# Two heads of a recurrent scan normed and gated at a time inside the scan's rounds, with half of a projection moved into its first rounds

## The reference, cut to what matters

```python
y_c, states_c = rwkv_scans(r_c, v_c, dirs_c, (zero, zero))   # both directions, 8 heads of 64
y_l, _ = rwkv_scans(r_l, v_l, dirs_l, states_c)
def rwkv_out(y, r, v, dirs, g, prm):
    mean = jnp.mean(y, axis=-1, keepdims=True)               # over the 64 of a head
    var = jnp.mean(jnp.square(y - mean), axis=-1, keepdims=True)
    yn = ((y - mean) * lax.rsqrt(var + LN_X_EPS)).reshape(B, L, RW_DIM) * prm['ln_w'] + prm['ln_b']
    bonus = jnp.sum(r * k_sum * prm['r_k'], axis=-1, keepdims=True) * v
    return ((yn + bonus.reshape(B, L, RW_DIM)) * g).astype(g.dtype)
out_l = jnp.concatenate([rwkv_out(...), o_l], axis=-1) @ prm['w_out']   # the same for the context
```

## Time and profile before

| | us |
|---|---|
| median of 3 runs (lowest, highest) | 2639.47 (2636.53, 2642.45) |
| the profiled execution, its own time | 2644.11 |
| its span in the profile | 2642.2 |
| PE, VectorE, ScalarE (ACT), GpSimd (POOL) busy, share of the span | 91%, 66%, 40%, 13% |
| granted TensorE clock, mean | 0.951 |

### The profile page before, as it was taken

The page is one execution under the profiler, slowest core; times in us unless marked ns, Lnnn a source line. Parts: engine busy times, 40 slices in busy tenths (PEclk is TensorE's granted clock), DMA queues, the critical chain, the costliest instruction groups (busy, mean ns, idle before and its releaser), DMA issues.

```text
span 2642.2 us, 38711 instructions
## 1 busy us (share of the span) xinstructions
PE 2392.0 (91%) x15040; PEld 1770.8 (67%) x15040; DVE 1755.9 (66%) x3346; ACT 1047.5 (40%) x2030; POOL 354.1 (13%) x541
## 2 busy tenths in 40 slices
PE   7899999799989799899998799987899998998996
PEld 3788888554878799633454577774477775767775
DVE  4775786576746788722757566665568884647886
ACT  4222222233331444411134243432357873346884
POOL 1111100110000211000200233331012210001220
PEclk9899999899999799999998799998989999998998
DMA  7555654241326478311010000000269993215995
GB/s 284 183 203 196 215 199 144 93 143 64 123 85 207 158 274 289 132 56 56 32 40 32 25 3 3 2 3 1 96 212 347 334 314 131 72 53 190 337 330 198
DMA packets 115062, 386.97 MB, mean 146 GB/s; under 512 B 20160, under 2 KB 22336, under 8 KB 114624
## 3 DMA queue, kind: packets, MB, share of 16 engines
q1 hardware_dynamic: 76640, 276.33, 29.8%
q0 software_dynamic: 34848, 95.47, 10.7%
q10 hardware_dynamic: 3392, 12.70, 1.2%
HBM read 389.66 MB, written 26.21 MB: 157 GB/s over the span
## 4 chain that ended last, share of the span: by engine, by line
PE 35%; DVE 14%; DMA 8%; ACT 6%; issue 3%; POOL 0%; DVEq 0%; ACTq 0%; SPq 0%; POOLq 0%
PE ps L143 34%; DMA RG<-in_w 6%; DVE moe1wl L152 2%; DVE moe0wl L152 2%; DMA AR<-in_a 2%; PE ps L146 1%; DVE f2wl L152 1%; ACT moe1wh L149 1%; ACT moe0wh L149 1%; DVE rwXX L152 1%; DVE rwMM L172 1%; DVE H L160 1%; DVE acc L160 1%; ACT rwa L149 1%; ACT f2wh L149 1%
## 5 line engine op out<-in xcount | busy, mean ns | idle before, releaser
L143 PE MATMUL ps<-H,RG 128*128 128x256 f32 (+2 forms) x1088 | 364.1, 491 | 14.0 <-ACT H L149 14.0
L160 DVE SCALAR_TENSOR_TENSOR acc<-AR,cs,acc 128x512 f32<-128x512 f32 x420 | 295.4, 746 | 48.8 <-DMA AR<-in_a 46.0
L143 PEld LDWEIGHTS ps<-H,RG 128*128 128x128 f32 (+1 forms) x1088 | 206.4, 193 | 156.2 <-issue 140.1
L152 DVE TENSOR_TENSOR moe0wl<-RG,moe0wh 128x1024 fp32r<-128x1024 f32 x144 | 173.2, 1219 | 44.1 <-ACT moe0wh L149 33.8
L149 ACT ACTIVATE moe0wh<-RG 128x1024 fp32r<-128x1024 f32 x144 | 150.9, 1061 | 75.4 <-DMA RG<-in_w 42.8
L199 POOL DMA_DIRECT2D AR<-in_a x152 | 82.1, 541 | 658.0 <-DVE acc L160 503.1
L152 DVE TENSOR_TENSOR moe1wl<-RG,moe1wh 128x1024 fp32r<-128x1024 f32 x120 | 144.4, 1219 | 26.9 <-ACT moe1wh L149 22.2
L149 ACT ACTIVATE f1wh<-RG 128x1024 fp32r<-128x1024 f32 x66 | 69.7, 1061 | 230.7 <-PE ps L143 230.6
L143 PE MATMUL ps<-f1hh,f1wh 128*128 128x512 f32 x352 | 142.9, 406 | 8.0 <-DVE f1hl L152 8.0
L149 ACT ACTIVATE moe1wh<-RG 128x1024 fp32r<-128x1024 f32 x120 | 126.1, 1060 | 49.7 <-DMA RG<-in_w 30.2
L143 PE MATMUL ps<-f1hl,f1wh 128*128 128x512 f32 x352 | 141.5, 402 | 0.0
(11 more groups left out here) (643 smaller groups left out, 5834.0 us busy)
## 6 DMA issues: line engine op xcount, KB each, us to landing
RG<-in_w SPq DMA_DIRECT2D x525, 512.0 KB
AR<-in_a POOLq DMA_DIRECT2D x152, 512.0 KB, 3.9
moe0back<-moe_outs ACTq DMA_DIRECT2D x4, 1024.0 KB, 8.0
CT<-in_consts ACTq DMA_DIRECT2D x1, 2546.0 KB, 12.6
X<-in_x ACTq DMA_DIRECT2D x1, 2048.0 KB, 11.7
moe_rows<-moe0ht POOLq DMA_DIRECT2D x4, 512.0 KB, 5.0
moe1back<-moe_outs ACTq DMA_DIRECT2D x2, 1024.0 KB, 5.9
X<-in_ctx ACTq DMA_DIRECT2D x1, 1024.0 KB, 5.7
```

Of the source, the lines that this page charges most:

```text
L143: return Silent() if self.e is None else self.e.matmul(out, lhs, rhs, start=start, stop=stop, skip_group_check=True)
L152: return Silent() if self.e is None else self.e.tensor_tensor(out, a, b, op)
L160: return Silent() if self.e is None else self.e.scalar_tensor_tensor(out=out, in0=a, scalar=s, in1=b, op0=op0, op1=op1)
```

## The change

- **Start.** `out1` is split: columns 0 to 3 stay ahead of the scan, columns 4 to 7 are multiplied by PE in rounds 0, 1, 2 and 4 and added by VectorE in rounds 1, 2, 3 and 5. The terms of the bonus are made by VectorE in round 0, its products in round 8, its multiplications in round 9. POOL no longer waits for `out1`.
- **Storage.** `ST` and the `MM` of set 1 get space of their own. In each set `EI` shares its space with `T1` and `KB` with `XX`; the masks and one `T1` go to the end of `rwa` and to `nv`. VectorE's first write into `XX` waits for ACT's copy of `kbt`.
- **Closing.** Each pair of heads is normed and gated in the rounds after its last unit, from rounds 146, 159, 165 and 175 on, one operation a round (`close_pe`, `close_act`, `close_dve`); for the last pair VectorE's operations follow each other in round 177. All squares are ACT's; the root table is loaded in round 157. The rounds end at 179 instead of 175.
- **Second outputs.** The router's part moves to rounds 149 and 150. In rounds 175 to 177 the first four columns of `out2` get their products of the first three pairs of heads (`late_pe`); the fourth follows after the scan (`led_pe`), then columns 4 to 7.

```diff
     NS, APART = 4, 5
+    CLOSE = [146, 159, 165, 175]
...
-        self.ST = self.OM[:, 0:2, :].rearrange("p d (j n) -> p d j n", j=4)
-        size = dict(EB=[P, 129], EI=[P, P], RA=[P, 256], KB=[P, 2, P], KBt=[P, 2, P], MM=[P, 2, 512], WU=[P, 2, P],
-                    XF=[P, 2, P], XX=[P, 2, 2, 64], T1=[P, 2, 64], sm=[P, 2])
+        self.ST = g.sb(st, "rwst", [P, 2, 4, P])
+        size = dict(EB=[P, 129], RA=[P, 256], KBt=[P, 2, P], MM=[P, 2, 512], WU=[P, 2, P], XF=[P, 2, P], XX=[P, 2, 2, 64],
+                    T1=[P, 2, 64], sm=[P, 2])
...
-            self.sets.append({k: g.sb(st, f"rw{k}{i}", s) for k, s in size.items() if i > 1 or k != "MM"})
-        self.sets[1]["MM"] = self.OM[:, 2:4, :]
+            self.sets.append({k: g.sb(st, f"rw{k}{i}", s) for k, s in size.items() if i < 3 or k != "T1"})
+        self.sets[3]["T1"] = g.NV[:, 384:512].rearrange("p (a n) -> p a n", a=2)
         for B in self.sets:
             B["MC"], B["ML"] = (B["WU"][:, q, :].rearrange("p (h n) -> p h n", h=2) for q in range(2))
-        self.LC = [g.sb(st, f"rwlc{d}", [P, len(LEVELS) - 1, 64]) for d in range(2)]
-        self.IC = g.sb(st, "rwic", [P, 64])
+            B["EI"] = B["T1"].rearrange("p a n -> p (a n)")
+            B["KB"] = B["XX"].rearrange("p q h n -> p q (h n)")
+        self.LC = [x.rearrange("p (l n) -> p l n", n=64) for x in (self.A[:, at:at + 384], g.NV[:, 0:384])]
+        self.IC = self.A[:, at + 384:at + 448]
...
-        self.run(e, self.unit_pe)
-        for f in range(4):
-            ps = g.banks.take(("rw mean", f))
-            for tok in g.banks.free(("rw mean", f)):
-                e.wait_ge(*tok)
-            e.wait_ge(*S.dve.at("scanned"))
-            e.matmul(ps[:, :], g.C("avg64"), self.YB[:, f, :], True, True).then_inc(*p.up(("mean", f)))
-        self.nyb.pe(e)
-        g2, tok_g = g.ws.tile(("rw_g2_2", ix, (0, P), (0, T)), P, T)
-        e.wait_ge(*tok_g)
-        for f in range(4):
-            ps = g.banks.take(("rw g2", f))
-            for tok in g.banks.free(("rw g2", f)):
-                e.wait_ge(*tok)
-            e.matmul(ps[:, :], g2[0][:, f * P:(f + 1) * P], self.SG[:, :], True, True).then_inc(*p.up(("g2", f)))
-        g.ws.settle("rw g2", p.now())
+        self.run(e, self.unit_pe, self.close_pe, amid)
...
-        self.nyb.act(e, [S.dve.at(("centred", 3))])
+        self.run(e, self.unit_act, self.close_act)
...
+    def bonus_terms_dve(self, e):
+        g, v, K = self.g, self.S.dve, self.K
+        e.wait_ge(*v.now())
+        e.tensor_tensor(K[:, :, :], self.KD[0][:, :, :], self.KD[1][:, :, :], ADD).then_inc(*v.up())
+        e.wait_ge(*v.now())
+        e.tensor_tensor(K[:, :, :], K[:, :, :], self.R[:, :, :], MUL).then_inc(*v.up())
+        e.wait_ge(*v.now())
+        e.tensor_tensor(K[:, :, :], K[:, :, :], bc(g.V("r_k", 0, 4), [P, 4, T]), MUL).then_inc(*v.up("bonus"))
...
     def pool(self, e):
-        for tok in needs:
-            e.wait_ge(*tok)
...
-        self.nyb.pool(e, [S.dve.at(("centred", 3))])
...
-    def run(self, e, unit):
-
-        running = []
-        for r in range(self.APART * (len(self.todo) - 1 + self.NS)):
+    def run(self, e, unit, close=None, beside=None):
+
+
+        running, closing = [], []
+        for r in range(self.CLOSE[-1] + 4):
...
+            if close is not None and r in self.CLOSE:
+                closing.append(close(e, self.CLOSE.index(r)))
+            for u in list(closing):
+                if next(u, "over") == "over":
+                    closing.remove(u)
+            if beside is not None:
+                beside(e, r)
+
+    def last(self, j):
+
+        return self.todo.index((3, 1, j))
+
+    def close_pe(self, e, j):
+
+        g, p, S, y = self.g, self.S.pe, self.S, self.YB[:, j, :]
+        ps = g.banks.take(("rw mean", j))
+        for tok in g.banks.free(("rw mean", j)):
+            e.wait_ge(*tok)
+        e.wait_ge(*S.dve.at(("out", self.last(j))))
+        e.matmul(ps[:, :], g.C("avg64"), y, True, True).then_inc(*p.up(("mean", j)))
+        yield from (None for _ in range((10, 3, 3, 1)[j]))
+        ps = g.banks.take(("rw squares", j))
+        for tok in g.banks.free(("rw squares", j)):
+            e.wait_ge(*tok)
+        e.wait_ge(*S.act.at(("square", j)))
+        e.matmul(ps[:, :], g.C("avg64"), self.squares[:, j, :], True, True).then_inc(*p.up(("squares", j)))
+        yield from (None for _ in range((5, 5, 5, 1)[j]))
+        if j == 0:
+            self.g2 = g.ws.tile(("rw_g2_2", (0,), (0, P), (0, T)), P, T)
+        w, tok_g = self.g2
+        e.wait_ge(*tok_g)
+        ps = g.banks.take(("rw g2", j))
+        for tok in g.banks.free(("rw g2", j)):
+            e.wait_ge(*tok)
+        e.matmul(ps[:, :], w[0][:, j * P:(j + 1) * P], self.SG[:, :], True, True).then_inc(*p.up(("g2", j)))
+        if j == 3:
+            g.ws.settle("rw g2", p.now())
+        yield
+
+    def close_act(self, e, j):
+        g, a, S = self.g, self.S.act, self.S
+        yield from (None for _ in range((2, 2, 2, 1)[j]))
+        e.wait_ge(*S.dve.at(("centred", j)))
+        e.activation(self.squares[:, j, :], self.YB[:, j, :], ACT.Square).then_inc(*a.up(("square", j)))
+        yield from (None for _ in range((9, 2, 2, 1)[j]))
+        if j == 0:
+            g.root_table(e)
+        e.wait_ge(*S.pe.at(("squares", j)))
+        e.activation(self.roots[:, j, :], g.banks.of(("rw squares", j))[:, :], ACT.Abs_reciprocal_sqrt,
+                     bias=g.C("eps64")).then_inc(*a.up(("root", j)))
+        yield
+
+    def close_dve(self, e, j):
+        g, v, S = self.g, self.S.dve, self.S
+        y, m, inv = self.YB[:, j, :], self.squares[:, j, :], self.roots[:, j, :]
+        apart = int(j < 3)
+        yield from (None for _ in range(apart))
+        e.wait_ge(*S.pe.at(("mean", j)))
+        e.wait_ge(*v.at(("out", self.last(j))))
+        e.tensor_tensor(y, y, g.banks.of(("rw mean", j))[:, :], SUB).then_inc(*v.up(("centred", j)))
+        g.banks.done(("rw mean", j), v.now())
+        yield from (None for _ in range((10, 3, 3, 2)[j]))
+        e.wait_ge(*S.act.at(("root", j)))
+        e.scalar_tensor_tensor(m, g.banks.of(("rw squares", j))[:, :], 64e-5, inv, ADD, MUL).then_inc(*v.up())
+        g.banks.done(("rw squares", j), v.now())
+        yield from (None for _ in range(apart))
+        e.wait_ge(*v.now())
+        e.scalar_tensor_tensor(m, m, -0.5, inv, MUL, MUL).then_inc(*v.up())
+        yield from (None for _ in range(apart))
+        e.wait_ge(*v.now())
+        e.scalar_tensor_tensor(inv, m, 1.5, inv, ADD, MUL).then_inc(*v.up())
+        yield from (None for _ in range(apart))
+        e.wait_ge(*v.now())
+        e.scalar_tensor_tensor(y, y, g.V("ln_w", j), inv, MUL, MUL).then_inc(*v.up())
+        yield from (None for _ in range(apart))
+        e.wait_ge(*v.now())
+        e.scalar_tensor_tensor(y, y, g.V("ln_b", j), self.V[:, j, :], ADD, ADD).then_inc(*v.up())
+        yield from (None for _ in range(apart))
+        e.wait_ge(*v.now())
+        e.wait_ge(*S.pe.at(("g2", j)))
+        e.tensor_tensor(self.R[:, j, :], y, g.banks.of(("rw g2", j))[:, :], MUL).then_inc(*v.up(("r", j)))
+        g.banks.done(("rw g2", j), v.now())
+        yield
 
...
+                e.wait_ge(*S.act.at(("kbt", n)))
...
+        self.amid = [0, 1, 2, 4]
...
-        for f in range(KT):
-            if f == KT - 2:
-                self.rwkv.bonus_pe(e)
+        for f in range(4):
             self.out1.one_pe(e, f)
+
+    def amid_pe(self, e, r):
+
+        if r in self.amid:
+            self.out1.one_pe(e, self.amid.index(r) + 4)
+        if r == 8:
+            self.rwkv.bonus_pe(e)
+        self.late_pe(e, r)
+
+    def late_pe(self, e, r):
+
+        if r == 149:
+            self.router.pe(e, 0)
+        if r == self.rwkv.CLOSE[3]:
+            self.lead = {}
+        if r >= self.rwkv.CLOSE[3]:
+            for f in {0: [0], 1: [1, 2], 2: [3], 3: []}[r - self.rwkv.CLOSE[3]]:
+                self.lead[f] = self.out2.bank(e, f)
+                for k in range(3):
+                    self.lead_one_pe(e, f, k)
+
+    def lead_one_pe(self, e, f, k):
+        s = self.out2.specs(f)[k]
+        w, tok = self.g.ws.tile(s[:4], s[4], s[5])
+        e.wait_ge(*tok)
+        e.wait_ge(*self.rwkv.S.dve.at(("r", k)))
+        return e.matmul(self.lead[f], w[0], self.rwkv.R[:, k, :], k == 0, k == 3)
+
+    def led_pe(self, e):
+        p = self.S.pe
+        for f in range(4):
+            self.lead_one_pe(e, f, 3).then_inc(*p.up(("out", f)))
+        self.g.ws.settle((self.S.name, "out", 3), p.now())
+
+    def late_dve(self, e, r):
+        if r == 150:
+            self.router.dve(e, 0)
+            self.out2.gate_dve(e)
 
     def attended_dve(self, e):
         self.out1.gate_dve(e)
         e.wait_ge(*self.SO.dve.now())
-        for f in range(KT):
-            if f == KT - 2:
-                self.rwkv.bonus_dve(e)
+        for f in range(4):
             self.out1.one_dve(e, f)
+
+    def amid_dve(self, e, r):
```

(73 more changed lines are left out.)

## The result

The changed kernel takes 2613.34 us (median of four runs, 2609.39 to 2615.44), the kernel before in the same comparison 2638.01 (four runs, 2636.53 to 2642.45): ratio 0.9898, 95% interval 0.9879 to 0.9916, so about 1% faster. The profiled execution of after took 2615.44 us, span 2613.6.

A forecast was written before the change was run, and what follows sets the result against it. PE was taken to bound the kernel. Start 9.4 gained, closing in the rounds 8.5 lost and behind the scan 25.3 gained make 26.2 us, so 2613.3 us beside 2639.5; range 2603 to 2627 (8 in 10).

The forecast's parts named there:

- Start: Ahead of the scan and in its first rounds: splitting out1 fills PE's hole; 9.4 us gained, bounds 5 and 15.
- POOL hidden: Ahead of the scan: POOL's masks and clearings, 5.9 us, are covered by other engines' work.
- the bonus: In round 8: four bonus products on PE, taken in full at 3.6 us lost.
- the clock's return: Units 1 to 5: PE is throttled less after a shorter idle stretch; 2.0 us gained.
- Closing in the rounds: Norm and gate of the first three pairs inside the scan's rounds: 8.5 us lost, bounds 4 and 17.
- the allotment: Closing inside the rounds: loss summed from separate engine terms, PE 3.2 and 2.2, router 0.6, DVE 1.3, ACT 1.2 us.
- Behind the scan: From last mean to the end of out2: PE stays the bound without stalls; 25.3 us gained, bounds 23 and 27.
- Squares between exponentials: ACT's squares from round 148: no table load of their own, 0 taken, 2.6 us kept for the range.
- the slower rival: In each of 32 units DVE's first write into XX waits for ACT's kbt copy: 2645 us, chance 0.03.
- Rival 1: In the scan's rounds: the closing is fully seen, 18 us lost instead of 8.5; 2623 us, chance 0.17.
- Rival 3: First units: the clock does not fall, 4.8 more; scan's end hides closing products, 3; 2606 us, chance 0.15.
- rival 2: First rounds: the early start brings nothing, bonus products double if the clock stays at half; 2623 us, chance 0.10.

The follow-up runs named there:

- no_bonus: Changed kernel with the four bonus products and their multiplications left out (bonus missing from the output): 2606.31 us, ratio 0.9862 to the kernel before.
- thin_all: Changed kernel with the first three pairs' closing products and DVE and ACT operations on 64 columns in place of 512: 2609.49 us, ratio 0.9894 to before.
- Experiment 2: Four variants of the changed kernel, the first three pairs' closing partly left out or thinned on PE, on DVE and ACT, or on all: ratios 0.9886 to 0.9904 to before.
- start_only: Kernel before with only the change's first rounds and storage; norm, gate and second outputs stay behind the scan: 2633.65 us, ratio 0.995 to before.

## Why the prediction was right, and where it was not

The total (2613.3 against 2613.34) is closer than its terms deserve, and that is luck. The gain was put at 26.2 us and measured at 24.7; the other 1.5 us are the median of before, 2639.5 in the prediction and 2638.0 beside the result. Of the three terms the two gains were put 1.1 us too small each and the loss 3.5 too small.

- **Start, 9.4 predicted, 10.5 measured.** The first level product 11.0 us early: 11.3. POOL hidden: yes. But the bonus was counted at 3.6 and costs 6.9, and the clock's return at 2.0 where 6.1 came (17.4 at unit 28 in no_bonus less 11.3). I had bounded the bonus by hiding (0) and by doubling at half clock (7.2) and taken the middle. The size came near the upper bound, but not by that road: the block itself ran at 1.00 in 3.60 us, and the price lies in what it holds up and in the clock behind it. Two terms missed by 3 and 4 us with opposite signs, so the 9.4 is near by luck; other traces of the same rounds have unit 28 up to 4.2 us earlier still. Units 1 to 5 took 46.6 us, just outside the 41 to 46 I gave.
- **Closing in the rounds, 8.5 predicted, 12.0 measured** (10.5 ahead at unit 28, 1.5 behind at the last mean). This is the mis-sized term. 8.5 of it are lost at full clock up to "last full"; that this equals the 8.5 predicted for the whole closing is chance. The other 3.5 lie behind, where the clock is at half for 6.8 us and the third pair's three Newton operations, its last two and its gate product (2.02 us, at 1827.68) stand among the last unit's. PE waits there behind the Newton operations:

```profile
1823.55 0.69 PE L143 MATMUL ps<-rwXX,rwMM 64*64 64x64 f32 x4 [1.33 <-DVE rwXF L152]
```

With all of that thinned (thin_all) 3.3 of the 3.5 come back. The step that failed is the allotment: PE's products 5.4, DVE 1.3, ACT 1.2, router 0.6 as separate terms. Experiment 2 shows that they can't be summed: PE's alone give back 2.5, DVE's and ACT's alone 2.3, both 5.9 of 8.5. DVE with ACT was put too low; of ACT's 1.2 for load and root the load makes 0.2, and of the router's 0.6 there is 0.2.
- **Behind the scan, 25.3 predicted, 26.4 measured.** PE full, no stall, the led fourths 13.0 us behind the mean (three led products stand ahead of them in the group at 1841.58) where I had 13.4. What I had a little high is the product: 39 of them took 33.6 us, 0.86 each, at full clock; my 0.89 held a slow head.
- **The side notes.** The Trainium skill's price for a switch of table, 2.66 us with a drain of 1.38 in it (ScalarE: Activation LUTs, What ACT_TABLE_LOAD costs), was set against the trace: the load took 1.28 us at 1794.66, right behind the activation ahead of it (1794.37, 0.28 us), the idle activation began at 1795.96, and no drain of 1.38 shows on either side. Squares between exponentials need no load: none stands in rounds 148 to 156. `XX` never waits for the `kbt` copy, so the slower rival had nothing to act on.
- **Rivals.** Rival 1 was half right: more of the closing was seen. Rival 3 had the size of the clock's return (6.1 instead of 2.0, with no bonus in the rounds), but its condition did not hold in after, where the clock was at 0.50 for 13.7 us, and a bonus as dear as in rival 2 took the gain back. Rival 2's outcome did not come: the start brought 10.5 us.

## What to carry to other kernels

Where rounds tie PE, DVE and ACT together, don't price added work as a share per engine: measure with all of it thinned, then one engine at a time. Here the single numbers summed to 4.8 us where both together gave 5.9. Try work moved out of a hole spread over the thin rounds one instruction at a time, not set down as a block: here that made four products free that cost 4.3 to 6.9 us as a block. And count marks from the last operation that both kernels share, for executions drift by more than the terms in question.

## What the runs showed of the hardware

TensorE's clock fell with PE never idle for long: in after it went from 1.00 to 0.50 at about 1495.7, and in the 6 us ahead of it PE was busy 3.28 us with 1.84 us as the longest wait. With the four products spread, PE was busy 4.99 and then 4.11 of 6 at the same marks and the clock stayed at 1.00.

The same instructions met different clocks. At the scan's end start_only lost 4.0 us in a fall that came 7 us sooner than in before. Behind the bonus block the clock came back after 13.6 to 13.7 us in six traces and after 3.4 in two, with the same instructions ahead of the fall, worth some 2.5 us by unit 5. A single trace's start is good to some 2 to 4 us for that reason, while the closing, at full clock, repeated to 0.1 us in the five traces that kept it.
